# Transpositions behind two norms split between the next chunks, token halves at the norms and at the end, and alternating PSUM banks in a delta-rule and state-space block

## The chip, the core and the metric

The kernel runs on one core of a Trainium2 chip. The core has five engines with a queue of instructions each: TensorE (PE in the trace, its weight loads PEld), VectorE (DVE), ScalarE (ACT), GpSimd (POOL) and SyncE (SP, which here only issues transfers). They meet at semaphores. TensorE reads the on-chip memory SBUF and writes the accumulator memory PSUM; VectorE and ScalarE read both. The metric is the device time of one execution in microseconds; lower is better.

## The reference

One sequence of 256 tokens of width 2048 goes through two layers, in float32. The first is modulated by a conditioning vector: a gated delta-rule mixer (16 query/key heads, 32 value heads), a layer norm, a gated feed-forward block (FFN), a layer norm. The second is a hybrid: an RMS norm, eight projections, a short convolution branch and a state-space branch (s5), their mix, an output projection, the residual, and a last RMS norm.

```python
mod = (cond @ mod_w[i] + mod_b[i])[:, None, :]
sh1, sc1, ga1, sh2, sc2, ga2 = jnp.split(mod, 6, axis=-1)
h = x * (1 + sc1) + sh1
y = gated_deltanet(h, ...)                  # ends with o @ gdn_w_out
x = layer_norm(ALPHA_DN * x + (1 + ga1) * y, ln_g[i, 0], ln_b[i, 0])
h = x * (1 + sc2) + sh2
y = swiglu(h, ffn_w_gu[i], ffn_w_down[i])
x = layer_norm(ALPHA_DN * x + (1 + ga2) * y, ln_g[i, 1], ln_b[i, 1])
...
h = rmsnorm(x, norm_g)
proj = jnp.einsum('bld,dn->bln', h, w_in)
v, bg, cg, za, u, zb, ga, gb = jnp.split(proj, SPLITS, axis=-1)
...
m = jax.nn.sigmoid(ga) * ya + jax.nn.sigmoid(gb) * yb
x = x + jnp.einsum('bld,de->ble', m, w_o)
return rmsnorm(x, final_g)
```

## The kernel before, in words

Every product is made to float32 accuracy from three products of shorter numbers: a weight and an activation are each split into a high part (`wh`, `hh`) and a low part (`wl`, `hl`), and high x high, high x low and low x high are summed in PSUM. Weights stream through four buffers in **chunks** of 2 x 128 rows by 512 columns. SyncE loads a chunk into `wr`, ScalarE copies its high part (`high`, L1582; in the delta loop `gh`, L1391), VectorE subtracts for its low part (`low`, L2059; in the delta loop GpSimd does it, L595), and TensorE multiplies. A chunk that gives tokens on partitions (`tchunk`) takes 12 matmuls of 512 columns, six for each half of 128 tokens; one that gives channels on partitions (`chunk`) takes 24 of 256 columns. The semaphores s_hc, s_lc and s_ck count high parts, low parts and used chunks. `stream` on ScalarE and VectorE runs three chunks ahead and has events hung between the chunks.

PSUM is four tensors of 1024 columns, two banks each: pg0, pg1, pd0, pd1.

**Delta loop.** The projections of head block g (8 blocks, 24 chunks each: q and k, then v, then z) run beside the delta rule of block g-1. Before each of most chunks TensorE takes one step of the delta rule, which waits for VectorE and ScalarE. q and k gather in pg0, v in pg1, z in pg0 again (in block 0 z goes to pd1). ScalarE copies z out at the turn to the next block (`z_out`, L1439), and the next block's first chunk waits for it, since it writes pg0 as well. VectorE and ScalarE run six of these blocks in a hardware loop, TensorE's are written out. VectorE also forms columns of the modulation from tiles of `mod_w` (L1818, L1820), which GpSimd's queue loads between its low parts.

**Output projection and first norm.** The 40 chunks of `w_out` (numbers 0 to 39, `CK_FF` = 40) fill four blocks of 512 output columns; the last is chunks 24 to 39 in pg1. Small work is hung between them: at chunk 38 TensorE transposes 16 tiles (`bbar`), which ScalarE copies (`prep3`). After chunk 39 TensorE spreads the modulation ga2 over the partitions (`row_of`, L1146), while VectorE scales the last block by ga1, adds the residual, takes the statistics and the mean and variance (`scaled`, `stats`, `mean_var`). ScalarE makes the inverse deviation from a logarithm and an exponential (`inv_std`), VectorE normalizes four blocks of 512 columns (L2256), TensorE transposes each (`flip`, 8 tiles a block, 32 in all, into pd0 and pd1 by turns), ScalarE scales and shifts them on the way out of PSUM (`lift`, L1662), and VectorE splits them into high and low (`split_up`, L2114 and L2115). Then the FFN's first chunk starts.

**Second norm.** The FFN's last down-projection ends in four blocks (`down_last`), each scaled, added and measured. Before each, VectorE makes two low parts, chunks of the hybrid's projection among them. Then follow inverse deviation, scale and shift in tokens (L2309, L2311), ScalarE's squares for the RMS norm (L1683), the second normalization (L2318), `flip`, `lift` and `split_up` as before. The hybrid's first 32 chunks (u and zb) are a hardware loop of two passes on TensorE and ScalarE; ScalarE counts up the loop's start semaphores after the last `lift`.

**End.** `w_o` is 32 chunks into pd0 and pd1 by turns. After the last chunk VectorE adds the last 512 columns of both token halves (L2437), ScalarE squares (L1763), VectorE sums (L2440), ScalarE takes the root, VectorE multiplies four parts of 1024 columns (L2445) and SyncE stores each.

What sets the order around the change is the order in which the code stands on each engine, and the semaphores; there is no planner.

## Time and profile before

| what | value |
|---|---|
| median of 3 runs | 2849.15 us (2848.85 to 2851.08) |
| the profiled execution | 2848.96 us, its span 2847.0 us |
| mean granted clock of TensorE | 0.986 of full speed |
| TensorE busy | 2720.7 us, 96% of the span |
| VectorE, ScalarE, GpSimd busy | 1949.3, 1208.2, 812.5 us |
| read from HBM | 548.19 MB, 193 GB/s over the span |

The span runs from the first to the last instruction of the traced execution. Busy times of the engines overlap. Where TensorE idles, the trace names the instruction that it waited for. A wait for several semaphores is put down to the one that came last.

### The profile page before, as it was taken

How to read it: one execution, taken by the hardware profiler on the slowest of the kernel's cores; microseconds unless marked ns; L12 is line 12 of the kernel's file. 1: busy time of each engine (PE TensorE's matmuls, PEld its weight loads, DVE VectorE, ACT ScalarE, POOL GpSimd, SP SyncE). 2: the span in 40 equal slices, each digit the busy share in tenths (PEclk: the TensorE clock that was granted, in tenths of full speed). 3: DMA queues.
4: the chain of work that ended last, by engine and by line, in shares of the span. 5: the costliest groups of instructions: out<-in, count | busy, mean ns of one | idle time of the engine just before them, and what ended most of it. 6: DMA issues, size and time to landing. Idle time of an engine off the chain costs nothing.

```text
span 2847.0 us, 51314 instructions
## 1 busy us (share of the span) xinstructions
PE 2720.7 (96%) x20214; PEld 2404.2 (84%) x20214; DVE 1949.3 (68%) x2285; ACT 1208.2 (42%) x1521; POOL 812.5 (29%) x554
## 2 busy tenths in 40 slices
PE   6999999999997999999999999969999999999998
PEld 4788988898895777888888888769899999999996
DVE  1377877787778677666666666676999898555554
ACT  2255455545544444333333333344333334433343
POOL 1066666666667510000000000001555552000000
PEclk8999999999999999999999999989999999999999
DMA  9866666676665666666665555535554555555554
GB/s 364 311 195 214 223 216 200 205 247 199 200 223 169 212 184 207 187 191 189 188 188 187 189 189 186 167 115 169 156 171 148 157 169 172 179 185 183 184 201 147
DMA packets 283920, 552.72 MB, mean 194 GB/s; under 512 B 16817, under 2 KB 54258, under 8 KB 282610
## 3 DMA queue, kind: packets, MB, share of 16 engines
q1 hardware_dynamic: 263632, 474.02, 52.7%
q0 software_dynamic: 19408, 76.06, 7.2%
q8 instruction: 130, 2.13, 0.3%
q10 hardware_dynamic: 722, 0.28, 0.0%
q14 instruction: 28, 0.23, 0.0%
HBM read 548.19 MB, written 2.10 MB: 193 GB/s over the span
## 4 chain that ended last, share of the span: by engine, by line
PE 79%; DVE 11%; ACT 4%; issue 2%; DMA 2%; POOL 1%; DVEq 0%; SPq 0%; ACTq 0%; POOLq 0%; PEld 0%
PE pg L1130 20%; PE pg L1117 14%; PE pg L821 13%; PE pd L1130 11%; PE pd L1117 7%; PE pg L812 4%; DVE wl L2059 2%; PE pd L736 2%; DMA arena<-in_mod_w 1%; DVE arena L2340 1%; PE pd L985 1%; DVE arena L2342 1%; PE pd L1003 1%; DVE arena L2335 1%; PE pg L842 1%
## 5 line engine op out<-in xcount | busy, mean ns | idle before, releaser
L2059 DVE TENSOR_TENSOR wl<-wr,wh 128x1024 fp32r<-128x1024 f32 x616 | 773.0, 1264 | 515.7 <-ACT wh L1582 512.5
L1582 ACT ACTIVATE wh<-wr 128x1024 fp32r<-128x1024 f32 x616 | 652.6, 1060 | 1004.8 <-PE pg L1117 344.6
L595 POOL TENSOR_TENSOR wl<-wr,wh 128x1024 fp32r<-128x1024 f32 x195 | 479.8, 2462 | 394.3 <-ACT wh L1391 394.1
L1117 PE MATMUL pg<-hh,wh 128*128 128x256 f32 x1536 | 438.4, 285 | 3.9 <-ACT arena L1700 2.5
L1117 PE MATMUL pg<-hl,wh 128*128 128x256 f32 x1536 | 434.6, 283 | 0.0
L1117 PE MATMUL pg<-hh,wl 128*128 128x256 f32 x1536 | 434.3, 283 | 0.0
L1391 ACT ACTIVATE wh<-wr 128x1024 fp32r<-128x1024 f32 x216 | 227.7, 1057 | 349.3 <-PE pg L821 219.9
L821 PE MATMUL pg<-hh,wh 128*128 128x256 f32 x1024 | 301.2, 294 | 14.8 <-ACT arena L1439 12.0
L1117 PEld LDWEIGHTS pg<-hh,wh 128*128 128x128 f32 x1536 | 294.4, 192 | 16.6 <-issue 13.6
L1820 DVE SCALAR_TENSOR_TENSOR arena<-arena,condt 128x512 f32<-128x512 f32 x240 | 282.4, 1177 | 32.4 <-DMA arena<-in_mod_w 26.9
L1117 PEld LDWEIGHTS pg<-hl,wh 128*128 128x128 f32 x1536 | 294.5, 192 | 0.0
L1117 PEld LDWEIGHTS pg<-hh,wl 128*128 128x128 f32 x1536 | 294.4, 192 | 0.0
L821 PE MATMUL pg<-hl,wh 128*128 128x256 f32 x1024 | 290.1, 283 | 0.0
L821 PE MATMUL pg<-hh,wl 128*128 128x256 f32 x1024 | 290.1, 283 | 0.0
L1130 PE MATMUL pg<-wh,hh 128*128 128x512 f32 x704 | 276.8, 393 | 0.0
L1130 PE MATMUL pg<-wl,hh 128*128 128x512 f32 x704 | 276.1, 392 | 0.0
L1130 PE MATMUL pg<-wh,hl 128*128 128x512 f32 x704 | 275.3, 391 | 0.0
L725 POOL COPY arena<-arena 128x256 f32 x8 | 6.4, 798 | 875.5 <-ACT arena L1700 875.5
L821 PEld LDWEIGHTS pg<-hh,wh 128*128 128x128 f32 x1024 | 196.5, 192 | 33.1 <-ACT arena L1439 14.6
L821 PEld LDWEIGHTS pg<-hl,wh 128*128 128x128 f32 x1024 | 196.8, 192 | 0.2 <-issue 0.2
L821 PEld LDWEIGHTS pg<-hh,wl 128*128 128x128 f32 x1024 | 196.6, 192 | 0.0
L1130 PEld LDWEIGHTS pg<-wh,hl 128*128 128x128 f32 x704 | 132.3, 188 | 29.4
(392 smaller groups left out, 5323.6 us busy)
## 6 DMA issues: line engine op xcount, KB each, us to landing
wr<-in_w_in SPq DMA_DIRECT2D x224, 512.0 KB, 3.9
wr<-in_ffn_w_gu SPq DMA_DIRECT2D x176, 512.0 KB, 4.4
wr<-in_gdn_w_in SPq DMA_DIRECT2D x128, 512.0 KB, 4.3
arena<-in_mod_w POOLq DMA_DIRECT2D x64, 1024.0 KB, 7.7
wr<-in_ffn_w_down SPq DMA_DIRECT2D x88, 512.0 KB, 3.6
arena<-in_mod_w SPq DMA_DIRECT2D x32, 1024.0 KB, 12.2
wr<-in_gdn_w_in SPq DMA_DIRECT2D x128, 256.0 KB, 2.9
wr<-in_gdn_w_out SPq DMA_DIRECT2D x56, 512.0 KB, 4.6
```

What stands on the lines that cost most here:

```text
L595: nc.gpsimd.tensor_tensor(wl[c % RING][:], wraw[c % 4], wh[c % RING][:].bitcast(F32), ALU.subtract)\
L736: return nc.tensor.transpose(dst, src, ident[0:n, 0:n])
L812: m = nc.tensor.matmul(halves(bank)[:, t, :], h_s[x][:, 2 * kp + k, t * P:(t + 1) * P], w[c % RING][:, k, :], skip_group_check=True, start ...
L821: m = nc.tensor.matmul(bank[:, n * T:(n + 1) * T], w[c % RING][:, k, n * P:(n + 1) * P], h_s[x][:, 2 * kp + k, :], skip_group_check=True, ...
L842: m = nc.tensor.matmul(halves(pg[g])[:, h, :], o_s[x][:, 2 * kp + k, h * P:(h + 1) * P], w[c % RING][:, k, :], skip_group_check=True, star ...
L985: m = nc.tensor.matmul(block(pd[par], *crossed(s, b, n)), lTb[r, n, r], Tc[r, n, :], start=True, stop=True)
L1117: m = nc.tensor.matmul(bank[:, n * T:(n + 1) * T], w[s][:, k, n * P:(n + 1) * P], act[x][:, k0 + k, :], skip_group_check=True, start=(firs ...
L1130: m = nc.tensor.matmul(halves(bank)[:, h, :], act[x][:, k0 + k, h * P:(h + 1) * P], w[s][:, k, :], skip_group_check=True, start=(first and ...
L1391: a(wh[c % RING][:], wraw[c % 4], ACT.Copy).then_inc(s_hi, 1)
L1582: a(wh[c % 4][:], wraw[c % 4], ACT.Copy).then_inc(s_hc, 1)
L1820: m = stt(out=dst, in0=mw[t % 2][:, k, :], scalar=condt[:, kk:kk + 1], in1=dst, op0=ALU.mult, op1=ALU.add)
L2059: v.tensor_tensor(wl[c % 4][:], wraw[c % 4], wh[c % 4][:].bitcast(F32), ALU.subtract).then_inc(s_lc, 1)
```

## The change

**Banks by turns in the delta loop.** `group_bank` gives the three groups of block g the banks 0, 1, 0 for odd g and 1, 0, 1 for even g from 2 on; block 0 is as before. A block's first chunk then waits for the convolution of the block before, and only its ninth for the z copy. ScalarE's and VectorE's hardware loops hold two blocks a pass.

**Token halves at the first norm.** The last four chunks of `w_out` are run for token half 0 first, all four, then for half 1. VectorE adds, measures and normalizes half 0 beside the second halves. ga2's rows move to chunk 30.

**Pieces at both norms.** The transposed blocks are cut into five pieces (0 and 1 are halves of block 0). TensorE transposes pieces 0 to 2 ahead of the first chunk of the next projection, piece 3 behind the first chunk and piece 4 behind the second. Low and high parts of the next chunks move in between. The hybrid's first loop is written out on TensorE and ScalarE, and the start semaphores are counted up ahead of the lifts.

**Token halves at the end.** The last four chunks of `w_o` run half 0 first; half 0 is squared, scaled and stored in part beside the second halves; the last store is 512 columns wide.

```diff
+LAST_OUT = 36
+OUT_PARTS = ((0, 0, 1024), (0, 1024, 2048), (1, 0, 1024), (1, 1024, 1536), (1, 1536, 2048))
+PIECES = ((0, 0, 2), (0, 2, 4), (1, 0, 4), (2, 0, 4), (3, 0, 4))
+def pieces_for(t):
+    return t + 1 if t < 2 else t // 2 + 2
+def first_bank(g):
+    return 0 if g == 0 else (g + 1) % 2
+        def group_bank(g, grp):
+            return pg[(first_bank(g) + grp) % 2]
...
@@ TensorE, gchunk @@
-                if c == 0 and not first_g:
+                if c == 0 and g == 1:
+                    pe.wait_ge(s_zo, 1)
+                    pe.wait_ge(s_cd, 1)
+                elif c == 0 and not first_g:
+                    pe.wait_ge(s_cd, g * 2)
+                if c == 8 and g == 1:
+                    pe.wait_ge(s_cd, 2)
+                elif c == 8 and not first_g:
                     pe.wait_ge(s_zo, g)
-                    pe.wait_ge(s_cd, g * 2 - 1)
-                if c == 8 and not first_g:
-                    pe.wait_ge(s_cd, g * 2)
...
@@ TensorE, the chunks of w_out @@
-                tchunk(0, 0, t, pg[g % 2], o_s, 2 * k, g >= 2 and k == 0, last)
+                if t < LAST_OUT:
+                    tchunk(0, 0, t, pg[g % 2], o_s, 2 * k, g >= 2 and k == 0, last)
+                elif t == LAST_OUT:
+                    for n in range(LAST_OUT, CK_FF):
+                        pe.wait_ge(s_lc, n + 5)
+                        m = half_chunk(n, 0, pg[1], o_s, 2 * out_chunk(n)[1], False, n == CK_FF - 1)
+                    m.then_inc(s_oh0, 1)
+                if t >= LAST_OUT:
+                    half_chunk(t, 1, pg[1], o_s, 2 * k, False, last).then_inc(s_ck, 1)
...
+                if t == 30:
+                    pe.wait_ge(s_ap, 4)
+                    pe.wait_ge(s_ev, 3)
+                    row_of(pg[0], 5 * KD)
+                    row_of(pd[1], 5 * KD + 8).then_inc(s_pp, 1)
...
-            flip(0, res)
+            flip(0, res, (0, 1, 2))
...
+            def first_need(n, src, t):
+                if t in (1, 2):
+                    flip(n, src, (t + 2,))
+                pe.wait_ge(s_hn, 5 * n + pieces_for(t))
...
-            flip(1, xs)
-            with pe.Fori(0, 2) as j:
+            flip(1, xs, (0, 1, 2))
+            for j in range(2):
                 for i in range(2):
                     pe.wait_ge(s_uz, j * 2 + (i + 1))
-                    group(j, 16, CK_HYB + 8 * i, pg[i], h_s, 8, lambda t: pe.wait_ge(s_hn, 5 + t // 2))
+                    group(j, 16, CK_HYB + 8 * i, pg[i], h_s, 8,
+                          (lambda t: first_need(1, xs, t)) if j == 0 and i == 0 else None)
...
@@ ScalarE @@
-            with act.Fori(0, NIT - 2) as j:
-                beside(j)
-                turn(j)
+            with act.Fori(0, (NIT - 2) // 2) as i:
+                for odd in range(2):
+                    beside(i * 2 + odd, odd)
+                    turn(i * 2 + odd, odd)
...
             def prep3():
-                act.wait_ge(s_pp, 5)
+                inv_std(1, 0, 1)
+                act.wait_ge(s_pp, 6)
...
-                for c in range(4):
-                    act.wait_ge(s_tr, 4 * n + c + 1)
+                for i, (c, first, end) in enumerate(PIECES):
+                    act.wait_ge(s_tr, 5 * n + i + 1)
...
+                    if i in (2, 3):
+                        high(0, 0, c0 + i - 2 + AHEAD)
...
+            for sem in (s_uz, s_uz, s_za, s_gb):
+                act.sem_inc(sem, 1)
-            inv_std(2)
+            inv_std(3, 0, TT)
...
-            with act.Fori(0, 2) as j:
-                stream(j, 16, CK_HYB, 16, {7: lambda: out_u(j), 15: lambda: out_zb(j)})
+            for j in range(2):
+                stream(j, 16, CK_HYB, 16, {7: lambda: out_u(j), 15: lambda: out_zb(j)}, 0 if j else 2)
...
@@ VectorE, first norm @@
+            def last_half(t):
+                bank, row, part = halves(pg[1])[:, t, :], ga1_row[:, 1536:D], res[:, t, 1536:D]
+                link(v.tensor_tensor(bank, bank, row, ALU.mult))
+                m = stt(out=part, in0=part, scalar=ALPHA, in1=bank, op0=ALU.mult, op1=ALU.add)
...
+                link(v.bn_stats(bst[:, t, 3, :], part))
+                mean_var(t, t + 1)
...
+            dve.wait_ge(s_oh0, 1)
+            last_half(0)
+            low(0, 0, CK_FF)
             dve.wait_ge(s_rs, 1)
             for c in range(4):
-                for t in range(TT):
...
+                normed(0, 512 * c, 512 * (c + 1))
+            low(0, 0, CK_FF + 1)
+            used(0, 0, CK_FF - 1)
+            last_half(1)
+            dve.wait_ge(s_rs, 2)
+            for c, first, end in PIECES:
+                normed(1, 512 * c + P * first, 512 * c + P * end).then_inc(s_xn, 1)
+            low(0, 0, CK_FF + 2)
+            split_up(0, (sg, hgt), CK_FF)
...
@@ VectorE, second norm @@
-            stream(0, 0, CK_FD, 8, {1 + 2 * n: (lambda n=n: down_last(n)) for n in range(4)})
+            stream(0, 0, CK_FD, 6, {1 + 2 * n: (lambda n=n: down_last(n)) for n in range(3)})
+            down_last(3)
...
+            low(0, 0, CK_HYB + 1)
             dve.wait_ge(s_x2, 4)
...
+            low(0, 0, CK_HYB + 2)
+            split_up(1, htmp, CK_HYB)
...
@@ the end: TensorE, ScalarE, VectorE @@
+            for c in range(CK_END - 4, CK_END):
+                pe.wait_ge(s_lc, c + 5)
+                m = half_chunk(c, 0, pd[1], m_s, 2 * (c - CK_O - 24), False, c == CK_END - 1)
+            m.then_inc(s_oh0, 1)
+            for c in range(CK_END - 4, CK_END):
+                half_chunk(c, 1, pd[1], m_s, 2 * (c - CK_O - 24), False, c == CK_END - 1).then_inc(s_ck, 1)
...
+            for t in range(TT):
+                squares_o(3, t, t + 1)
+                act.sem_inc(s_sq, 1)
+                act.wait_ge(s_mv, 4 + t)
+                link(a(rs[:, t:t + 1], mv[:, t, 0:1], ACT.Ln, scale=1.0 / D, bias=cst[:, 0:1]))
+                a(rs[:, t:t + 1], rs[:, t:t + 1], ACT.Exp, scale=-0.5).then_inc(s_rs, 1)
...
+            dve.wait_ge(s_oh0, 2)
+            add_half(0)
+            mean_square(0)
             dve.wait_ge(s_be, 16)
...
+            final(0)
+            used(0, 0, CK_END - 1)
+            add_half(1)
+            final(1)
+            mean_square(1)
+            for i in range(2, len(OUT_PARTS)):
+                final(i)
```

TensorE at the turn from block 2 to block 3: `pg0<-wh,hh` and `pg0<-hh,wh` name the bank written and the two operands. Before, the last rows of block 2 and the first of block 3:

```order
L812 MATMUL pg0<-wh2_59,hh_53 128x512
L812 MATMUL pg0<-wl2_63,hh_53 128x512
L812 MATMUL pg0<-wh2_59,hl_54 128x512
L821 MATMUL pg0<-hh_53,wh0_57 128x256
L821 MATMUL pg0<-hl_54,wh0_57 128x256
```

and after:

```order
L833 MATMUL pg1<-wh2_59,hh_53 128x512
L833 MATMUL pg1<-wl2_63,hh_53 128x512
L833 MATMUL pg1<-wh2_59,hl_54 128x512
L842 MATMUL pg0<-hh_53,wh0_57 128x256
L842 MATMUL pg0<-hl_54,wh0_57 128x256
```

No instruction moved; z, which the last rows of the block form, now lies in the bank that the next block's first rows leave alone.

VectorE at the first norm, from the last low part before the statistics to the first split. `wl<-wr,wh` is a low part, the rows `128x512 x8` are the normalization, `hh` and `hl` the split. Before:

```order
L2059 TENSOR_TENSOR wl_63<-wr,wh_59 128x1024
L2101 TENSOR_TENSOR pg<-pg,arena 128x1024
L2246 SCALAR_TENSOR_TENSOR arena<-arena,pg 128x2x512
L2105 BN_STATS arena<-arena 128x6 x2
L2109 BN_AGGR arena<-arena 128x2 x2
L2256 TENSOR_SCALAR arena<-arena 128x512 x8
L2114 CAST hh<-arena 128x1024
```

and after, from the statistics of half 0 on:

```order
L2321 BN_STATS arena<-arena 128x6
L2166 BN_AGGR arena<-arena 128x2
L2116 TENSOR_TENSOR wl_61<-wr,wh_57 128x1024
L2327 TENSOR_SCALAR arena<-arena 128x512 x4
L2116 TENSOR_TENSOR wl_62<-wr,wh_58 128x1024
L2314 TENSOR_TENSOR pg<-pg,arena 128x512
L2315 SCALAR_TENSOR_TENSOR arena<-arena,pg 128x512
L2321 BN_STATS arena<-arena 128x6
L2166 BN_AGGR arena<-arena 128x2
L2327 TENSOR_SCALAR arena<-arena 128x256 x2
L2327 TENSOR_SCALAR arena<-arena 128x512 x3
L2116 TENSOR_TENSOR wl_63<-wr,wh_59 128x1024
```

The same arithmetic stands twice at half the width, with the low parts of three chunks between its steps.

VectorE ahead of the second norm, the last two blocks of the down projection: `pd<-pd,arena` scales a block. Before:

```order
L2101 TENSOR_TENSOR pd<-pd,arena 128x1024
L2287 TENSOR_TENSOR arena<-arena,pd 128x2x512
L2105 BN_STATS arena<-arena 128x6 x2
L2059 TENSOR_TENSOR wl_62<-wr,wh_58 128x1024
L2059 TENSOR_TENSOR wl_63<-wr,wh_59 128x1024
L2101 TENSOR_TENSOR pd<-pd,arena 128x1024
L2287 TENSOR_TENSOR arena<-arena,pd 128x2x512
```

and after:

```order
L2158 TENSOR_TENSOR pd<-pd,arena 128x1024
L2372 TENSOR_TENSOR arena<-arena,pd 128x2x512
L2162 BN_STATS arena<-arena 128x6 x2
L2158 TENSOR_TENSOR pd<-pd,arena 128x1024
L2372 TENSOR_TENSOR arena<-arena,pd 128x2x512
L2162 BN_STATS arena<-arena 128x6 x2
L2166 BN_AGGR arena<-arena 128x2 x2
```

The two low parts between the blocks are gone from here; one stands behind the four pairs that scale and shift in tokens, the other behind the second normalization.

## Rows read from the trace of the kernel before

**Rows 1.** The page: span, section 1, and a line of section 5 (columns: busy us, mean ns).
```profile
span 2847.0 us, 51314 instructions
...
PE 2720.7 (96%) x20214; PEld 2404.2 (84%) x20214; DVE 1949.3 (68%) x2285; ACT 1208.2 (42%) x1521; POOL 812.5 (29%) x554
...
L1582 ACT ACTIVATE wh<-wr 128x1024 fp32r<-128x1024 f32 x616 | 652.6, 1060 | 1004.8 <-PE pg L1117 344.6
```

**Rows 2.** Waits of TensorE over the span: us in total, times, longest.
```profile
PE pg L821 <- ACT arena L1439: 12.0, 6, 2.0
...
PE pg L1117 <- ACT arena L1700: 2.5, 1, 2.5
```

**Rows 3.** Timelines of TensorE and VectorE at turns: start us, us, instruction, [idle before].
```profile
266.32 0.39 PE L821 MATMUL pg<-hh,wh 128*128 128x256 f32 x1 [2.01 <-ACT arena L1439]
...
269.29 1.88 PE L916 MATMUL pd<-arena,ones 128*128 128x512 f32 x4
...
378.17 0.49 DVE L1818 TENSOR_SCALAR arena<-arena,condt 128x512 f32<-128x512 f32 x1 [0.31 <-DMA arena<-in_mod_w]
...
400.60 1.95 DVE L1820 SCALAR_TENSOR_TENSOR arena<-arena,condt 128x512 f32<-128x512 f32 x2 [1.16 <-DMA arena<-in_mod_w]
```

**Rows 4.** TensorE's longest wait in the last delta block, 859 to 965.
```profile
PE pd L934 <- DVE arena L1933: 6.7, 1, 6.7
```

**Rows 5.** Timelines at the first norm: TensorE, VectorE, ScalarE.
```profile
1100.68 1.95 PE L1146 MATMUL pg<-ident,modt 128*128 128x128 f32 x16
1102.46 1.95 PE L1146 MATMUL pd<-ident,modt 128*128 128x128 f32 x16
...
1114.14 1.06 PE L736 MATMUL pd<-ident,arena 128*128 128x128 f32 x8 [0.76 <-ACT arena L1662]
1114.96 0.48 PE L1130 MATMUL pg<-wh,hh 128*128 128x512 f32 x1
...
1104.64 1.42 DVE L2105 BATCH_NORM_STATS2 arena<-arena 128x6 f32<-128x512 f32 x2
...
1107.17 3.74 DVE L2256 TENSOR_SCALAR arena<-arena 128x512 f32<-128x512 f32 x8 [0.69 <-ACT arena L1648]
...
1106.60 0.30 ACT L1647 ACTIVATE arena<-arena,cst 128x2 f32<-128x2 f32 x1 [0.21 <-DVE arena L2109]
...
1110.23 3.76 ACT L1662 ACTIVATE arena<-pd,arena 128x256 f32<-128x256 f32 x8 [3.10 <-PE pd L736]
```

**Rows 6.** Timelines at the second norm: VectorE, then TensorE.
```profile
1857.81 2.36 DVE L2059 TENSOR_TENSOR wl<-wr,wh 128x1024 fp32r<-128x1024 f32 x2
1860.09 1.23 DVE L2101 TENSOR_TENSOR pd<-pd,arena 128x1024 f32<-128x1024 f32 x1
...
1877.20 3.26 DVE L2318 TENSOR_SCALAR arena<-arena 128x512 f32<-128x512 f32 x8 [1.91 <-ACT arena L1687]
1881.74 0.69 DVE L2114 CAST hh<-arena 128x1024 fp32r<-128x1024 f32 x1 [1.28 <-ACT arena L1660]
...
1878.13 5.27 PE L736 MATMUL pd<-ident,arena 128*128 128x128 f32 x24 [20.30 <-DVE arena L2318]
...
1885.90 0.38 PE L1117 MATMUL pg<-hh,wh 128*128 128x256 f32 x1 [1.27 <-ACTq L1692]
```

**Rows 7.** A stretch of 1 us: each engine's busy us (instructions), then PEclk, DMA share, GB/s.
```profile
1882.00:1883.00 1.00, 1.00 (x6) 1.00 (x7) 0.97 (x2) 1.00 (x4) 0.00 (x0) 0.57 0.00 0
```

**Rows 8.** ScalarE's table load ahead of the second Silu of the hybrid block.
```profile
1977.89 1.28 ACT L1700 ACT_TABLE_LOAD   x1 [1.83 <-PE pg L1117]
```

**Rows 9.** The end: chain of waits, VectorE's timeline, and the DMA issues.
```profile
2814.93 20.19 PE pd L1130 x88
...
2837.21 0.73 ACT arena L1763 x2
...
2838.77 4.87 DVE L2445 SCALAR_TENSOR_TENSOR arena<-arena,xT 128x1024 f32<-128x1024 f32 x4 [0.60 <-ACT arena L1770]
...
out<-arena SPq DMA_DIRECT2D x4, 512.0 KB, 2.8
```

More of the change, by code:

```diff
@@ L573, in _ @@
                 loads(0, 0, CK_O + 8 * g, w_o, 512 * g, 8)
-            for i in range(2 * TT):
+            for i, (t, first, end) in enumerate(OUT_PARTS):
                 sp.wait_ge(s_fin, i + 1)
-                t, half = i // 2, slice((i % 2) * 1024, (i % 2 + 1) * 1024)
-                sp.dma_start(out[0, t * P:(t + 1) * P, half], res[:, t, half]).then_inc(s_out, 16)
-            sp.wait_ge(s_out, 32 * TT)
+                sp.dma_start(out[0, t * P:(t + 1) * P, first:end], res[:, t, first:end]).then_inc(s_out, 16)
+            sp.wait_ge(s_out, 16 * len(OUT_PARTS))
         @block.gpsimd
@@ L804, in gchunk @@
                 pe.wait_ge(s_low, g * NCH + (c + 5))
-                bank, first, last = pg[grp % 2], kp == 0, kp == 7
-                if first_g and grp == 2:
-                    bank = pd[1]
+                bank, first, last = pd[1] if first_g and grp == 2 else group_bank(g, grp), kp == 0, kp == 7
                 if grp == 2:
@@ L1198, in _, with flip @@
                     m.then_inc(s_pp, 1)
-            def flip(n, src):
-                for c in range(4):
-                    pe.wait_ge(s_xn, 4 * n + c + 1)
+            def flip(n, src, pieces):
+                for i in pieces:
+                    c, first, end = PIECES[i]
+                    pe.wait_ge(s_xn, 5 * n + i + 1)
                     if c == 1 and n == 0:
@@ L1206, in flip @@
                     if c >= 2:
-                        pe.wait_ge(s_hx, 4 * n + c - 1)
-                    for k in range(4):
+                        pe.wait_ge(s_hx, 5 * n + c)
+                    for k in range(first, end):
                         for h in range(TT):
@@ L1569, in beside, with turn @@
                     pass
-            def turn(j, more=None):
-                z_out(j + 1)
+            def turn(j, odd, more=None):
+                z_out(j + 1, group_bank(1 + odd, 2))
                 if more:
@@ L1582, in high, with stream @@
                 a(wh[c % 4][:], wraw[c % 4], ACT.Copy).then_inc(s_hc, 1)
-            def stream(j, per, c, n, events={}):
-                for t in range(n):
+            def stream(j, per, c, n, events={}, start=0):
+                for t in range(start, n):
                     if not (isinstance(j, int) and c + t + AHEAD >= CK_END):
@@ L1914, in _ @@
             squares(0)
-            for _ in conv(0, 1):
+            for _ in conv(0, 1, group_bank(0, 1)):
                 pass
@@ L2105, in stats, with mean_var @@
                     link(v.bn_stats(bst[:, t, g, :], res[:, t, 512 * g:512 * (g + 1)]))
-            def mean_var():
-                for t in range(TT):
+            def mean_var(first=0, end=TT):
+                for t in range(first, end):
                     m = v.bn_aggr(mv[:, t, :], bst[:, t].rearrange("p a b -> p (a b)"))
```

195 lines of the change are left out of this document (100 added, 95 removed).

## The prediction, made before the changed kernel had run

> **What bounds the kernel now.** I read the share table first: TensorE is busy for 96% of a span of 2847.0 us [rows 1]. So an edit pays only where TensorE stands still, or behind its last matmul. The table of waits names these places. The reader should see in it one line that counts six equal waits, 12.0 us together, of a projection matmul for ScalarE's copy of a PSUM bank at L1439, and one of 2.5 us for the Silu at L1700 [rows 2]. The timelines give the rest: both norms, where TensorE waits for a chain over VectorE and ScalarE, and the end. I took each in turn and followed the chain instruction by instruction. "Chunk" is one k-pair of a weight block.
>
> **Turns of the delta loop: 12.0 us.** At a turn, ScalarE copies the z block out of pg0, and the next projection, which writes pg0 too, starts at 266.32 after 2.01 us of idle behind that copy [rows 3]. After the change the next block writes the other bank, which the convolution left long before; the copy is asked for only eight chunks later. A chunk lasts 269.29 - 266.32 = 2.97 us [rows 3], so the copy has over 20 us. In six turns (into blocks 2 to 7) the wait goes; the turns into block 1 and into the output projection keep theirs, as the latter starts on pg0, which holds z. Sum: 6 x 2.0 = 12.0 us.
> What is late next? TensorE now comes 2.0 us earlier to VectorE's results, but the first mod_w tile is issued behind GpSimd's low part of chunk 2, which hangs on ScalarE's z copy and its next weight copy, neither of which moves. VectorE already waited 0.31 us for that tile at 378.17 and will wait 2.3 [rows 3]. So for some 20 us VectorE runs with up to 2 us less of a lead. At 400.60 it waits 1.16 us for a tile whose issue hangs on TensorE's chunks [rows 3]: there the whole schedule is 2 us earlier and the lead is back. I count no loss. The bounds are 0 and 12 us given back. Loop bodies on ScalarE and VectorE are twice as long with half the passes; I take that at nothing, covered by the same eight chunks on ScalarE.
>
> **First norm: 1.2 us, less the clock.** Before: the last chunk ends at 1100.68, where the ga2 rows begin, and the first FFN matmul is at 1114.96 [rows 5], so 14.3 us. The rows (16 matmuls, until 1104.4) and all 32 transpositions lie within it. After, with T0 the end of the four first halves:
> - The second halves take 24 x 0.229 = 5.5 us (88 matmuls in 20.19 us, [rows 9]) and 16 transpositions of bbar 1.9 us between them: T1 = T0 + 7.4.
> - VectorE on half 0: multiply and add at 512 columns are half of 1.23 [rows 6], statistics 0.71, aggregate 0.2: T0 + 2.3. ScalarE takes inv_std only behind the weight copy of chunk 41, which waits for chunk 37's second half: 2.75 + 1.06 [rows 1] and two small ops of 0.3 and 0.2 [rows 5], T0 + 4.4. Then four normalizations of 0.47 [rows 5] and a low part of 1.2 [rows 6]: T0 + 7.6. That is just behind T1, so half 0 costs no more than 0.2 us.
> - Half 1: 2.3 + 0.6, five pieces in 1.9, the low part of chunk 42 1.2 (it stands ahead of the split), the split of the first piece, half of 0.69 + 1.23 [rows 6], 1.0. Transposition and ScalarE's lift of that piece (two of eight that take 3.76, [rows 5]) end before. FFN starts at T1 + 0.2 + 7.0, some 7.3.
> - Exposed besides: the ga2 rows, moved to chunk 30, 3.7 us, which VectorE had hidden; and two groups of eight transpositions behind FFN chunks 0 and 1, 1.07 each at full clock [rows 5], 2.1 together. They wait for nothing: their pieces were normalized before, and the pd bank they use was lifted.
> 7.3 + 3.7 + 2.1 = 13.1 against 14.3. Bounds: -1.5 (a loss) and +2 us.
>
> **Second norm: 3.0 us, less the clock.** Before, two low parts start at 1857.81 and hold VectorE 2.36 us, so the last down block is scaled at 1860.09, though TensorE was done at 1857.8 [rows 6]. After, they stand behind the second normalization's arithmetic and behind the pieces: the whole chain comes 2.2 us earlier. The first moved one fills the 1.9 us in which VectorE waits for ScalarE [rows 6]; the second, 1.2 us, delays the split: pieces start at 1875.0 instead of 1877.20, take 3.5, low part 1.2, split of the half piece 1.0: 1880.9. The hybrid projection started at 1885.90, behind the lift of all four and ScalarE's semaphore increments, which have moved ahead of it [rows 6]. Gain 5.0, minus two groups of transpositions now between chunks, 2.0: 3.0. Bounds 0 and 4.
>
> **The clock at the norms: -2 us together.** Before the first matmul behind either norm TensorE has stood still for some time. The granted clock is then its lower level, 0.50 of full speed (1.2 GHz), and at the second norm it rises only during 1882-1883, of which it averages 0.57 [rows 7], after transpositions from 1878.13 on [rows 6]. So far the low clock touched only transpositions. Now fewer of them stand before the first chunk and idle time lies between, so part of a chunk may run at 1.2 GHz. A chunk at half speed costs 2.8 to 2.9 us more; I take 1.0 us at each norm, bounds 0 and 2.9.
> The Trainium skill ("TensorE: Matmul & The Clock Gate", What's actually happening) says that throttled is the default state and that activity releases it. The trace agrees: full clock returns only after TensorE has worked. By that rule the thinner row of transpositions releases it later; by the start of work alone it would be as before and the 2 us would stay.
>
> **Table load: 1.3 us.** The u/zb loop is written out twice on ScalarE, and in its order the second Silu has no table load. Before, the load at 1977.89 takes 1.28 us [rows 8], inside TensorE's wait of 2.5 us [rows 2]. Bounds 1.2 and 1.4.
> The skill's page "ScalarE: Activation LUTs" (What ACT_TABLE_LOAD costs) gives about 2.66 us, a drain included; by it the sum would be 1.4 us larger. The trace has the load end and the Silu begin at once, so I keep 1.3.
>
> **End: 3.6 us.** Before, the last matmul ends at 2814.93 + 20.19 = 2835.12, and the fourth final multiply at 2838.77 + 4.87 = 2843.64 [rows 9]: 8.5 us, then 3.4 to the span's end. After, token half 0 is squared, scaled and half stored during the last 5.5 us of matmuls. Behind the end: add 0.6; final(1), which stands ahead of the mean, 1.3; reduce 0.2 (ScalarE's squares, 0.73 [rows 9], end meanwhile); two small ops 0.5; multiplies 1.3 + 0.6 + 0.6, and 0.15 of hops: 5.25. The last store is 256 KB instead of 512, which landed in 2.8 [rows 9], and fewer queue before it: 3.1 instead of 3.4. Gain 3.3 + 0.3. Bounds 3.0 and 4.3.
>
> **Sum** against the profiled run's own 2848.96 us: 12.0 + 1.2 + 3.0 - 2.0 + 1.3 + 3.6 = 19.1, so 2829.9. The median of the shown runs, 2849.15, lies 0.2 above: 2830.
>
> **Rivals.**
> - *Slow chunks at both norms.* The clock stays at 1.2 GHz for the whole first chunk: 5.7 us instead of 2.0, 2834. For it: over 4 us of transpositions before the full clock at the second norm [rows 6, 7]. Against: 16 transpositions still stand ahead of the first chunk, and 24 were enough [rows 6].
> - *No clock loss,* and the first norm at its better bound: 2827.
> - *The turn's gain is eaten by VectorE.* The late mod_w tile pushes the chain until TensorE waits for it again, the place changed but not the time: 12 us back, 2842. For it: 0.31 us of wait there already. Against: not one TensorE wait on VectorE in those six blocks, and the idle 1.16 us at 400.60.
> - *Slower: the delta chain becomes TensorE's bound.* In the last block, where chunks are shorter, TensorE waits 6.7 us for one result of VectorE's [rows 4]. If the shifted VectorE brought that wait into each of six blocks, 6 x 6.7 = 40 us: 2870. It decides from (19.1 + 5.7) / 6 = 4.1 us of new waits per block on. Against: only 2 us are shifted.
>
> **Chances.** 0.2% is 5.7 us, about what a measurement of this kernel can tell from no change. Forecast 2830 with 0.65 (2828 to 2832), slow chunks 0.15, no clock loss 0.10, VectorE eats it 0.05 (still faster by 0.25%), slower 0.03, and 0.02 for that case with the norms giving nothing as well, within 0.2%. Faster 0.95, same 0.02, slower 0.03. Range 2825.5 to 2836.
>
> **What the changed profile would show.** Right: no TensorE wait on the z copy except into block 1 and the output projection, and each block 2.0 us shorter; eight transpositions after chunks 0 and 1 behind each norm; TensorE's wait at the second norm near 18 us, not 20.3 [rows 6], then short ones; one L1755 table load; the last final multiply 5.2 us behind the last matmul. A granted clock of 0.50 in the first chunk's stretch would set the norm terms lower. Wrong would be: new TensorE waits on VectorE's triangular steps after the turns, or VectorE's half 0 far behind T1, which would leave the first norm a loss.

## The result, and where the time went

| kernel | median | against the kernel before |
|---|---|---|
| before | 2849.28 us (20 runs) | |
| after | 2853.72 us (20 runs) | 1.0017, 95% interval 1.0011 to 1.0023 |

The change makes the kernel slower by 0.17%, at the edge of what can be told from nothing. 2830.0 had been forecast, 24 us below. One of the 20 runs of the kernel after took 4457.06 us at a mean granted clock of 0.556, and the ratio leaves it out. The profiled execution took 2852.55 us, its span is 3.6 us longer than before. First the page of the kernel after, to hold against [rows 1]: busy us, share, instructions.

```profile
span 2850.6 us, 51255 instructions
...
PE 2725.0 (96%) x20214; PEld 2408.0 (84%) x20214; DVE 1982.7 (70%) x2297; ACT 1203.9 (42%) x1522; POOL 807.1 (28%) x554
```

TensorE has the same instructions as before. VectorE has 12 more, because steps were cut into parts, and is busy 33 us longer. It got no more arithmetic to do, so the time must lie inside instructions that stand still. The waits of TensorE come next (us in total, times, longest), to hold against [rows 2, 4, 6].

```profile
PE pd L955 <- DVE arena L1989: 21.8, 7, 6.7
PE pd L755 <- DVE arena L2405: 17.9, 1, 17.9
PE pd L1321 <- DVE arena L2434: 13.0, 8, 1.9
...
PE pd L1006 <- DVE arena L2019: 1.6, 3, 0.5
PE pg L1138 <- ACT arena L1755: 1.1, 1, 1.1
```

The six waits on the z copy (12.0 us) are gone, as forecast. In their place the Gram products (L955) wait in each of six blocks, 2.3 to 2.6 us each, for VectorE's scaling of q and k (L1989). The seventh wait of that row is the 6.7 us of [rows 4].

Following one instruction after another at the same point of the program in both traces gives a ledger. The lag is how much later the kernel after is there.

| point of the program | lag, us | step |
|---|---|---|
| z copy into block 1 | 0.0 | |
| first chunk of the output projection | +10.3 | turns +10.3 |
| its chunk 29 | +8.9 | the lower clock lasts longer in before, -1.4 |
| its last chunk | +12.5 | ga2 rows +3.5 |
| first Silu of the FFN | +9.4 | first norm -3.1 |
| last down-projection chunk | +10.5 | longer low clock in after, +1.1 |
| end of the first 32 hybrid chunks | +7.1 | second norm -3.4 |
| behind the second Silu | +5.7 | table load -1.4 |
| last matmul | +7.1 | state loop +1.4 |
| last final multiply | +3.8 | end -3.3 |
| end of the span | +3.6 | end -0.2 |

Only the first step is far from its forecast, by 22 us. It shows in one instruction: the first of the three copies (of 8, 8 and 16 numbers a partition) with which VectorE fetches the convolution's taps for the next block (`taps`; L1844 before, L1900 after). These are the rows of that line in both kernels (min/median/max ns, first and last start).

```profile
L1844 DVE COPY arena<-vc x8: 173/1376/1519, 16.4 to 767.9; 128x8 f32 x6, 128x8 f32<-128x8 f32 x2
```

```profile
L1900 DVE COPY arena<-vc x8: 171/5982/6096, 16.4 to 774.8; 128x8 f32 x6, 128x8 f32<-128x8 f32 x2
```

The copy needs 0.17 us, took 1.4 before and takes 6.0 now. The timelines at the turn into block 3 tell why. Before (start us, us; VectorE, then GpSimd):

```profile
372.60 1.37 DVE L1844 COPY arena<-vc 128x8 f32 x1 [0.18 <-DVE arena L1927]
...
371.51 2.42 POOL L595 TENSOR_TENSOR wl<-wr,wh 128x1024 fp32r<-128x1024 f32 x1
374.92 3.12 POOL L595 TENSOR_TENSOR wl<-wr,wh 128x1024 fp32r<-128x1024 f32 x1 [1.00 <-ACT wh L1391]
```

After (VectorE, GpSimd, TensorE):

```profile
372.37 5.98 DVE L1900 COPY arena<-vc 128x8 f32 x1 [0.18 <-DVE arena L1983]
378.95 1.23 DVE L1989 TENSOR_TENSOR arena<-arena 128x1024 f32<-128x1024 f32 x1
...
372.03 1.54 POOL L608 DMA_DIRECT2D arena<-in_mod_w  x2
373.59 4.72 POOL L614 TENSOR_TENSOR wl<-wr,wh 128x1024 fp32r<-128x1024 f32 x2
...
380.24 2.72 PE L955 MATMUL pd<-arena 128*128 128x128 f32 x16 [2.58 <-DVE arena L1989]
```

Before, the copy ended at 373.97, when GpSimd's low part ended (373.93) and GpSimd then had to wait 1.00 us for ScalarE's next high part. After, it ended at 378.35, when the second of two low parts ended (378.31). At this turn TensorE's chunks are at the same time in both traces, within 0.25 us. Relative to them the z copy is 2.0 us later, since TensorE no longer waits for it. GpSimd's chain hangs on the z copy, so these low parts start 2.1 us later; the next high part hangs on TensorE and starts 0.2 us earlier. So the idle microsecond between two low parts, through which the copy had slipped, is closed. The same shift also lets the copy begin ahead of the row of low parts, during the issue of the two loads, instead of beside a low part; no run here separates the two. The q/k scaling behind the copy comes 2.6 us later than TensorE now wants it.

The Trainium skill ("SBUF — State Buffer", Who interferes with whom) says that VectorE and GpSimd share one pair of ports and that whoever starts first holds it for the whole instruction; on VectorE's side this concerns copies in a mode that uses both ports, and steps with two operands from SBUF while GpSimd reads SBUF. The trace agrees on who is blocked. By that rule the copy would have been let through behind the first low part, at about 376.0; it stood until the second had ended. What held the copy from 372.37 to 373.57, beside the issue of two loads, no run here shows: in e4 below it took 0.45 us beside the same issue.

The wait also has a price in the clock. The granted clock fell to 0.50 for about 3 us around the Gram products in three of the six blocks (from 279.0, 381.4 and 582.8 on), where the kernel before stays at 1.00; here is one stretch of 1 us from the kernel after (busy us of PE, PEld, DVE, ACT, POOL, then the clock, DMA share, GB/s).

```profile
382.00:383.00 1.00, 1.00 (x7) 1.00 (x7) 0.96 (x3) 0.72 (x1) 0.00 (x0) 0.50 0.92 335
```

The 16 matmuls at 380.24 take 2.72 us where the same 16 took 1.95 before. These three blocks fall back by 2.0 to 2.2 us each, the other three by 1.1 to 1.4.

The last delta block has the same picture, before and after alike. Here VectorE's scaling of q and k itself is in the queue behind GpSimd (VectorE, GpSimd's last of four subtractions in a row from 879.72 on, TensorE):

```profile
879.35 10.76 DVE L1989 TENSOR_TENSOR arena<-arena 128x1024 f32<-128x1024 f32 x1 [4.97 <-ACT arena L1518]
...
886.69 2.33 POOL L614 TENSOR_TENSOR wl<-wr,wh 128x1024 fp32r<-128x1024 f32 x1
...
890.16 1.23 PE L955 MATMUL pd<-arena 128*128 128x128 f32 x4 [6.72 <-DVE arena L1989]
```

A step of 1.2 us took 10.8. VectorE is not always held for the whole row, though. Further on in the same block of the kernel before, the masking pair gets in between two of GpSimd's subtractions that stand back to back:

```profile
885.60 4.22 DVE L1953 TENSOR_TENSOR arena<-arena,m1t 64x512 f32<-64x512 f32 x2
...
886.40 2.87 POOL L595 TENSOR_TENSOR wl<-wr,wh 128x1024 fp32r<-128x1024 f32 x1
889.23 2.86 POOL L648 TENSOR_TENSOR ol<-arena,oh 128x1024 fp32r<-128x1024 f32 x1
```

The pair ends at 889.82, half a microsecond behind the end of the first of them, and the second takes 2.86 us instead of 2.4. The six copies and the scaling in the kernel after all began while GpSimd was issuing loads, this pair beside a subtraction; but in e3 the last block's scaling began beside one too and stood for 9.07 us, through three more. What decides between the two cases is open.

The 10.8 us step is behind the 6.7 us row which the prediction quoted [rows 4], without asking how long the instruction waited for had taken.

### The profile page after: what moved, and what is told of

Same layout as the page of the kernel before. It is cut to its first block, busy times and chain, and to the rows that moved or that the text cites. A ratio compares the mean times of both kernels' runs of the same rounds, so it can differ in the third digit from the quotient of the medians.

```text
span 2850.6 us, 51255 instructions
## 1 busy us (share of the span) xinstructions
PE 2725.0 (96%) x20214; PEld 2408.0 (84%) x20214; DVE 1982.7 (70%) x2297; ACT 1203.9 (42%) x1522; POOL 807.1 (28%) x554
## 4 chain that ended last, share of the span: by engine, by line
PE 79%; DVE 13%; DMA 2%; issue 2%; ACT 1%; POOL 1%; DVEq 0%; SPq 0%; ACTq 0%; POOLq 0%; PEld 0%
PE pg L1149 20%; PE pg L1138 14%; PE pd L1149 12%; PE pg L842 10%; PE pd L1138 7%; PE pg L833 5%; DVE wl L2116 2%; DMA arena<-in_mod_w 2%; PE pd L755 2%; DVE arena L1900 1%; DVE arena L1876 1%; DVE arena L2428 1%; PE pd L1006 1%; DVE arena L2430 1%; PE pd L1024 1%
## 5 line engine op out<-in xcount | busy, mean ns | idle before, releaser
L1149 PEld LDWEIGHTS pg<-wh,hh 128*128 128x128 f32 x704 | 132.6, 188 | 31.4 <-DVE hl L2172 2.1
```

What stands on the lines that cost most here:

```text
L1149: m = nc.tensor.matmul(halves(bank)[:, h, :], act[x][:, k0 + k, h * P:(h + 1) * P], w[s][:, k, :], skip_group_check=True, start=(first and ...
```

## The experiments

### e1 and e2: the two halves of the change apart

e1 is the kernel before with `group_bank`, its waits and the doubled loops. e2 is the kernel after with this undone:

```diff
 def first_bank(g):
-    return 0 if g == 0 else (g + 1) % 2
+    return 0
...
-                elif c == 0 and not first_g:
-                    pe.wait_ge(s_cd, g * 2)
+                if c == 0 and not first_g:
+                    pe.wait_ge(s_zo, g)
+                    pe.wait_ge(s_cd, g * 2 - 1)
...
```

> The kernel before with only the turn part of the change: banks alternate from block to block, with the waits and the doubled loops that go with it; norms, table load and end as before. Theory 'blocked copy': in the changed kernel each of six blocks loses 3.6 us (a wait of 2.6 us for VectorE's q/k scaling, 0.3 and 0.6 us behind it) against 2.0 us gained at the z copy, so about +10 us here: 2859.5 (2858 to 2861), with VectorE's first tap copy of a block at 6.0 us instead of 1.4. By my prediction's own sum this kernel would be at 2837. If the loss came from the norm parts instead, it would be at 2837 as well.

> The changed kernel with the banks fixed as before and the projection's waits on z and on the convolution as before; the doubled loop bodies stay. From the two traces the other parts should be worth: first norm -0.2, second norm with the last down block -3.1, table load 0 net, end -3.5, together -6.8: 2842.5 (2841.5 to 2844). Six tap copies at 1.4 us again, six waits of 2.0 us on the z copy back. If doubled loop bodies cost something, it is slower than that by their price (my prediction took it at nothing).

Measured: e1 2859.81 us, ratio 1.0039 (1.0025 to 1.0052); e2 2842.45 us, ratio 0.9973 (0.9964 to 0.9983). Both within 0.4 us of what was expected. In e1 the row of the tap copy reads as in the kernel after:

```profile
L1855 DVE COPY arena<-vc x8: 173/5992/6129, 16.5 to 774.8; 128x8 f32 x6, 128x8 f32<-128x8 f32 x2
```

So the banks cost 10.4 us by themselves, the rest of the change is worth 7.0, and the doubled loop bodies, which e2 kept, cost nothing: in its trace the six blocks are within 0.1 us of the kernel before.

### e3: the copies moved away

```diff
+            link(taps(1))
...
-                if mods:
-                    done(taps(it + 1))
-                else:
-                    dve.sem_inc(s_v, 1)
+                dve.sem_inc(s_v, 1)
...
                 for h in range(VH):
                     m = stt(out=rhs1[:, h, :], ...)
                 done(m)
+                if more:
+                    link(taps(it + 2))
```

> The changed kernel with the three tap copies of a block moved on VectorE from the block's start to behind the rhs1 step of the block before, where VectorE is idle for 6.9 us. Theory 'the copy itself is slow' (its dynamic address, not what runs beside it): the whole turn gain is back, 2832. Theory 'blocked by GpSimd': the q/k scaling, which reads two SBUF operands, takes the copy's place, starts while GpSimd issues the two mod_w loads and stands still until the two low parts behind them end, so the block's wait shrinks only from 2.6 to about 1.9 us: 2850 (2847 to 2852), with a q/k scaling of over 6 us in the trace. Theory 'late mod_w tile': 2853, no change.

Measured: 2847.33 us, ratio 0.9992 (0.9983 to 1.0001), at the lower end of the second theory's range. The next block's rows show it (VectorE, GpSimd): the scaling of q and k now stands where the copy stood.

```profile
470.15 6.97 DVE L1987 TENSOR_TENSOR arena<-arena 128x1024 f32<-128x1024 f32 x1 [0.24 <-ACT arena L1518]
...
471.30 4.73 POOL L614 TENSOR_TENSOR wl<-wr,wh 128x1024 fp32r<-128x1024 f32 x2
```

It ends 1.1 us behind GpSimd's row, about its own length of 1.2. The copy itself is not slow: the step that takes its place ahead of that row of low parts is held as well. The waits at L955 fell from 21.8 to 15.8 us, of which the last block gave 1.7, and in the six blocks the clock fell once instead of three times.

### e4 and e5: GpSimd leaves a gap, VectorE untouched

```diff
                 for t in range(2):
                     mod_load(it * 8 + 32, t)
+                if not o_low:
+                    pool.wait_ge(s_v, it * len(VO) + VO["qkn"])
```

GpSimd's low parts behind the two loads wait for VectorE's scaling of q and k.

e5 has the wait without the `if`, so in the last block too.

> The changed kernel with one wait more, on GpSimd: in the seven loop blocks it starts the low part behind the two mod_w loads only when VectorE's q/k scaling of that block is done. VectorE's program is untouched. Theory 'blocked by GpSimd': the tap copy takes under 1.5 us, the q/k scaling 1.2, the new wait of the gram products is gone and all 3.6 us a block come back, 2832 (2831 to 2836). Theory 'the copy itself is slow': it still takes 6.0 us and the low parts now come behind it, 2854 or more. Theory 'late mod_w tile': 2853, since no load moves.

Measured: 2837.63 us, ratio 0.9963 (0.9949 to 0.9977). One wait added, on an engine that TensorE hardly waits for, wins 16 us against the kernel after. VectorE's copy and scaling (first two rows), and GpSimd behind them:

```profile
468.17 0.45 DVE L1902 COPY arena<-vc 128x8 f32 x1 [0.16 <-DVE arena L1985]
...
469.21 1.23 DVE L1991 TENSOR_TENSOR arena<-arena 128x1024 f32<-128x1024 f32 x1
...
481.19 4.60 DVE L2011 TENSOR_TENSOR arena<-arena,m1t 64x512 f32<-64x512 f32 x2
```

```profile
470.63 7.08 POOL L614 TENSOR_TENSOR wl<-wr,wh 128x1024 fp32r<-128x1024 f32 x3 [1.24 <-ACT wh L1445]
479.97 2.40 POOL L614 TENSOR_TENSOR wl<-wr,wh 128x1024 fp32r<-128x1024 f32 x1 [2.26 <-ACT wh L1445]
```

The copy takes 0.45 us, the scaling 1.23, and the wait at the Gram products is gone. It came out 5.6 us above the 2832 expected and outside the range. The trace names a wait that fits: the masking pair (L2011) falls beside a low part and takes 4.60 us, where the same pair took 1.63 in the kernel before and 4.34 in the kernel after. Here TensorE waits for it:

```profile
PE pd L989 <- DVE arena L2011: 9.1, 7, 1.3
```

In this trace the clock does not fall in the six blocks, and each is 0.9 us shorter than before: 5.4 us are won of the 12.0 forecast.

> The kernel with the one wait on GpSimd (low parts behind the two mod_w loads wait for VectorE's q/k scaling), now in the last delta block as well. In that block the q/k scaling took 10.8 us instead of 1.2 beside a row of GpSimd's subtractions without a gap, and TensorE waited 6.7 us for it, before and after the change alike. Theory 'blocked by GpSimd': it takes under 1.5 us there too, the 6.7 us wait goes and nothing takes its place: 6 to 7 us below the run with the gap in the loop blocks alone, 2831 (2828 to 2834). Theory 'that wait has another cause' (ScalarE's exponents, chunks of the output projection): no difference, 2837.6.

Measured: 2835.68 us, ratio 0.9953 (0.9939 to 0.9966). In the last block the scaling takes 1.23 us at 865.51 and its wait is gone. But 2835.68 is outside the expected range, and the intervals of e4 and e5 overlap, so no gain of e5 over e4 is shown. GpSimd is late with the low parts now (2.4 us in e4, 5.3 here):

```profile
PE pg L864 <- POOL wl L614: 5.3, 3, 2.5
```

TensorE's waits in the last block are 2.8 us shorter than in e4, yet the block is 1.1 us longer in the trace; more of its matmuls run at the lower clock.

### e6: a second gap, and e7: TensorE kept busy at the first norm

e6 has the gap of e5, the copies of e3, and ahead of the low part of chunk 6:

```diff
+                    if t == 4:
+                        pool.wait_ge(s_v, it * len(VO) + VO["lm"])
                     low(it + 1, t + 2)
```

> The gap in all blocks, the tap copies moved into VectorE's idle 6.9 us of the block before, and a second wait on GpSimd: the low part of chunk 6 waits for VectorE's masking of the Gram blocks (the pair of 64x512 multiplies), which in the run with one gap took 4.6 us for two beside GpSimd and which TensorE then waited for 1.3 us in each of six blocks. Theory 'blocked by GpSimd': these waits go (8 us) with the 6.7 of the last block: 2823 (2820 to 2827), the masking pair at 1.7 us. Rival 'GpSimd becomes late': held back 2.8 us longer, it is late with the low part of chunk 6 and TensorE waits for that instead: 2831.

Measured: 2841.99 us, ratio 0.9978 (0.9969 to 0.9987), worse than with one gap. The masking pair takes 1.39 us, as meant. But three low parts then run in a row, 7.99 us, and TensorE waits longer on the levels of the triangular inverse behind it, which nobody had expected:

```profile
PE pd L1027 <- DVE arena L2028: 15.0, 8, 2.3
```

e7 is e6 with these transpositions of no use:

```diff
+            pe.wait_ge(s_ev, 4)
+            fill(16)
             flip(0, res, (0, 1, 2))
+            fill(14)
```

> The kernel with both gaps and the moved tap copies, plus 30 transpositions of no use on TensorE in its idle time at the first norm (16 ahead of the row of 16 useful ones, 14 behind it), into a bank that is free. Nothing they write is read. In the changed kernel the granted clock fell to 0.50 at 1122 us and stayed there until 1125.3, so the first FFN chunk lasted 4.3 us instead of 2.7. If the clock follows TensorE's idle time ahead of it, the chunk is at full speed and 1.5 us are won against the kernel without them; in the time that is 0.05%, below what the comparison can tell, so the trace decides: mean granted clock of the first chunk 1.00 against 0.6 or so. If the clock fell for something else, the chunk stays at 4.3 us and the time is up to 0.3 us longer.

Measured: 2842.58 us, ratio 0.9977 (0.9967 to 0.9986), no difference in the time, as expected. What is left are the rows of TensorE and the granted clock. After (TensorE; then stretches of 1 us with busy us of PE, PEld, DVE, ACT, POOL, the clock, DMA share, GB/s):

```profile
1117.14 1.94 PE L755 MATMUL pd<-ident,arena 128*128 128x128 f32 x16 [3.73 <-DVE arena L2327]
1120.94 0.50 PE L1149 MATMUL pg<-wh,hh 128*128 128x512 f32 x1 [1.86 <-DVE hl L2172]
...
1122.00:1123.00 1.00, 1.00 (x4) 0.81 (x3) 0.96 (x2) 0.51 (x1) 0.00 (x0) 0.56 1.01 426
1123.00:1124.00 1.00, 1.00 (x4) 0.72 (x3) 1.00 (x2) 0.00 (x0) 0.00 (x0) 0.50 1.00 420
```

With the fillers:

```profile
1112.75 1.69 PE L758 MATMUL pg<-ident 128*128 128x128 f32 x14
1114.84 0.50 PE L1152 MATMUL pg<-wh,hh 128*128 128x512 f32 x1 [0.39 <-DVE hl L2182]
...
1115.00:1116.00 1.00, 1.00 (x5) 0.82 (x6) 0.97 (x3) 1.00 (x2) 0.00 (x0) 1.00 0.97 410
1116.00:1117.00 1.00, 1.00 (x6) 0.82 (x5) 0.96 (x2) 0.36 (x1) 0.00 (x0) 1.00 1.03 434
```

From the first FFN chunk's start to that of the second group of transpositions behind it took 8.1 us after, 7.4 in e6 and 6.5 in e7. The lower level cost 1.6 us in the kernel after. In e7 no stretch between 1104 and 1122 is below 1.00, which fits a clock that follows TensorE's idle time. But it is one trace of each kernel, and the low stretch moves by itself: in e6, the nearest kernel without the fillers, it lies at 1106 to 1112.8, over the transpositions and the start of the chunk. So the cause is not shown.

### e8: the table load alone

The u/zb loop written out twice in the kernel before (`for j in range(2)` on TensorE and ScalarE), in one execution.

> The kernel before with one edit: the two passes over u and zb written out twice on TensorE and on ScalarE. One look, for the trace. My prediction: the table load of 1.3 us inside TensorE's wait of 2.5 us goes and 1.3 us are won to the end. Theory from the two traces: the Silu's wait shrinks to 1.1, but the first state products wait for VectorE, which does not come earlier, so the 1.4 us are back by the first quarter of the state loop: waits on VectorE's L2346 of 13.0 to 13.5 us instead of 11.8, and a span of 2847 instead of 2845.6.

Measured: 2845.91 us, span 2844.0. The Silu's wait is 1.1 us, but my theory fell: the waits on L2346 stayed at 11.9 us,

```profile
PE pd L1277 <- DVE arena L2346: 11.9, 8, 2.0
PE pd L1117 <- ACT arena L1742: 1.7, 1, 1.7
PE pg L1117 <- ACT arena L1700: 1.1, 1, 1.1
```

and the 1.4 us gained at the Silu were still there at the end of the state loop. Most of the other 1.7 us of the span arose at 1006 to 1009, where the kernel before still ran at a clock of 0.50 and e8 at 1.00; the 1.5 us less of waiting in the one row of [rows 4] (5.2 us here) were lost again to the clock within the same block. So in this one trace the prediction's term holds. What took 1.4 us back in the kernel after is something else: TensorE waits 1.75 us for VectorE at 2093.89, where it had waited 0.24. (A fall of the granted clock at 2013 to 2016 costs 1.5 us, but the kernel before has one like it at 2060 to 2063.) e2 has the same wait of 1.75 us, at 2190.21. Why it came, no run here shows.

### e9 to e12: the order on VectorE, the gap without the change, the gap again

e9 is e5 with VectorE's half sums of the mod_w tiles one step later in each loop block (`if t: mods(j * 8 + 32, t - 1)`); e10 has e3's copies as well; e11 is the kernel before with e5's gap; e12 is e5 once more.

> The changed kernel with GpSimd's gap in all blocks and one edit on VectorE: in the loop blocks each half sum of a mod_w tile comes one step later. In the run with the gap alone VectorE stood 3.7 us ahead of its decay-and-mask multiply for the block's first mod_w tile, so the masking pair of 64x512 fell beside a low part, took 4.6 us instead of 1.6, and TensorE waited 1.3 us in each of six blocks (7.8). Theory: with the tile behind that pair the pair runs before GpSimd's next low part and the 7.8 us are won: 2828 (2825 to 2831) against the gap kernel beside it. Rival: the sums, one step later, are late for the loads they release, or the two-operand steps collide with another low part: TensorE waits elsewhere on VectorE or on a tile and the time stays at 2835 or above.

Measured: 2905.13 us, ratio 1.0191 (1.0178 to 1.0205), the rival's case and 70 us above its bound:

```profile
PE pd L756 <- DVE arena L2033: 38.5, 20, 3.4
...
PE pd L1065 <- DVE arena L2041: 10.8, 7, 2.4
PE pd L1037 <- DVE arena L2033: 10.2, 7, 1.6
```

TensorE waits on nearly every level of the inverse. The sums are the same instructions as in e5; a step later they stand ahead of those that TensorE waits for.

> The same with the tap copies moved into VectorE's idle time of the block before. The q/k scaling comes 1 us earlier, so GpSimd is held for less; TensorE waits for neither after the gap, so the theory expects no more than 1 us: 2827.5 (2825 to 2831). If the copies still hurt where they stand, it is 2 us or more ahead of the kernel without this edit.

Measured: 2900.69 us, ratio 1.0183 (1.0170 to 1.0196). With e9's order the base is lost, so it tells little of the copies.

> The kernel before with GpSimd's gap in all blocks and nothing of the change. TensorE did not wait for VectorE in its loop blocks, and the 2.0 us on the z copy stay, so nothing is to be won there; in the last block the 6.7 us wait goes and 2.9 us of waiting for the low parts come, as in the changed kernel. Theory: 2849.4 - 3.8 = 2845.6 (2843 to 2848), so the gap is worth about 4 us here against 18 beside the alternating banks. Rival: the gap is an improvement by itself, of the same size without the change: 2832. A gap that pushes the low parts onto VectorE's masking pair here too would cost up to 8 us back: 2849 or more.

Measured: 2856.34 us, ratio 1.0023 (1.0014 to 1.0032). The gap makes the kernel before slower and the kernel after faster: with the z wait in place TensorE does not wait for VectorE in the six blocks, and holding GpSimd for 3.3 us pushes its low parts onto the masking pair. All six z copy waits stay (12.0 us), and four new ones come:

```profile
PE pg L822 <- ACT arena L1440: 12.0, 6, 2.0
...
PE pd L967 <- DVE arena L1954: 5.1, 4, 1.3
```

In the trace the six blocks lose 9.6 us, 5.1 of them in these waits and most of the rest in three falls of the granted clock to 0.50; the last block wins 6.5.

> The kernel with the gap in all blocks once more, on the chip of the three others, so that they can be compared with it: 2835.7 as before (2833 to 2838).

Measured: 2835.69 us, ratio 0.9947 (0.9934 to 0.9960), the same as e5. This is the version that beats both kernels, by 14 us over before. Against e2, which leaves the banks out, it is 6.8 us faster, so the banks pay only together with the gap.

## Why the prediction was wrong

**Turns: forecast -12.0, measured +10.3.** The wait on the z copy went as forecast, 2.0 us in six blocks. The step that failed is "What is late next?", which asked it only of the mod_w tile and ended in "I count no loss". It followed VectorE's semaphores and left out that VectorE and GpSimd hinder each other without any. Moving TensorE 2 us earlier while GpSimd's chain stayed closed the idle microsecond between two low parts. Against the 12.0 us gained stand 22.3 us lost in the six blocks: 15.1 of waiting at the Gram products, 1.6 in three waits at a step behind them (L1006), and 5.6 in which TensorE ran slower, most of it at the granted clock of 0.50. That GpSimd would meet VectorE there could have been read before: 1.37 us for a copy of 8 numbers, ending where the low part ended, and 10.8 us for a step of 1.2. e1 shows the size, e3 that it isn't the copy, e4 that it is GpSimd's row. As to the mod_w tile, in the kernel after VectorE has no idle time ahead of its first mod_w step of these blocks. In e4 it waits 2.7 to 3.7 us for the tile and TensorE for nothing at the Gram products; whether that delay put the masking pair beside a low part, e9 was meant to show and could not.

**The rival that came nearest** is "Slower: the delta chain becomes TensorE's bound", which had 0.03. It named the kind of wait and the row, but had 6.7 us a block and 2870. By the prediction's own sum the gain is gone from 19.1 / 6 = 3.2 us a block on, and at 4.1 the kernel is slower by 0.2%; it was 3.7, a third more than the 2.8 of waits alone because of the clock, which this rival did not count. Its counter-argument, "only 2 us are shifted", failed because a shift of 2 us can change a duration by 4.6.

**First norm: forecast -1.2 and a clock loss of 1.0.** Measured are +3.5 for the ga2 rows (forecast 3.7) and -3.1 for the rest (forecast -4.9 + 1.0). The first FFN chunk starts 7.5 us behind the last chunk of the output projection, as worked out (7.3). The lower clock cost 1.6 us instead of 1.0 and is most of the difference: the norm part is 0.4 us of loss instead of 0.2 of gain.

**Second norm: forecast -3.0 and a clock loss of 1.0; measured -3.4.** TensorE's wait is 17.9 us ("near 18"), the hybrid starts 23.0 us behind the last down chunk instead of 28.1. The clock loss did not come:

```profile
1886.25 3.67 PE L755 MATMUL pd<-ident,arena 128*128 128x128 f32 x16 [17.89 <-DVE arena L2405]
1891.39 0.36 PE L1138 MATMUL pg<-hh,wh 128*128 128x256 f32 x1 [1.47 <-issue]
...
1889.00:1890.00 1.00, 0.93 (x5) 0.52 (x3) 1.00 (x2) 0.13 (x2) 0.00 (x0) 0.50 0.00 0
1890.00:1891.00 1.00, 0.00 (x0) 0.00 (x0) 0.97 (x3) 1.00 (x3) 0.00 (x0) 0.94 0.00 0
```

The 16 transpositions ran at 0.50, and the clock rose in the idle time ahead of the first chunk. The term of 2.0 us for both norms was right in sum (1.6) by luck, with one norm above its 1.0 us and one below.

**Table load: forecast -1.3, measured -1.4** at its place, and in the one execution of e8 it lasts.

**End: forecast -3.6, measured -3.5.** VectorE's rows and the stores, to hold against [rows 9]:

```profile
2842.26 0.69 DVE L2530 TENSOR_TENSOR arena<-arena,pd 128x512 f32<-128x512 f32 x1 [1.84 <-PE pd L1149]
...
2844.81 2.61 DVE L2539 SCALAR_TENSOR_TENSOR arena<-arena,xT 128x1024 f32<-128x1024 f32 x3 [0.60 <-ACT arena L1826]
...
out<-arena SPq DMA_DIRECT2D x3, 512.0 KB, 2.6
out<-arena SPq DMA_DIRECT2D x2, 256.0 KB, 2.7
```

The last multiply ends 5.20 us behind the last matmul (2842.22), where 5.25 had been worked out, and the span ends 3.2 us later (forecast 3.1).

The range of 2825.5 to 2836 was built from the bounds of the small terms. The largest term had bounds of 0 and 12 us given back and none for a loss, so it was the one that needed a row for its worst case.

## What to carry to other kernels

Before an engine's wait is taken away, look at how long the instructions of its partners last against the shortest of their kind, not only at who waits for whom: one that takes eight times its length and ends with another engine's instruction is a wait that no semaphore shows. Count also what a new wait does to the granted clock behind it. A shift of 2 us opens or closes such windows, in either direction, so a gain at one engine should be priced with the whole rows of VectorE and GpSimd laid side by side at their new times. A wait added to an engine with slack can be worth more than one removed from the bottleneck, but only beside the change that needs it.

## What the runs showed of the hardware that had not been expected

- A VectorE instruction blocked by GpSimd can stay blocked beyond the end of the GpSimd instruction: until two low parts had ended (6.0 us for a copy of 8 numbers that takes 0.17), or four (10.8 us for a step of 1.2). It need not: the masking pair at 885.60 in the kernel before got in between two subtractions in a row.
- GpSimd is hindered less the other way: a low part took 2.4 us alone and 2.9 to 3.1 where VectorE was at work first.
- Small steps suffer as much as large ones: the sum of four modulation columns (128x4) took 1.63 us at 362.87 in the kernel before, beside a low part, and 0.16 us at 477.37 in e9 without one.
- The granted clock fell to 0.50 inside running matmuls, 1.2 us after they had begun behind 1.9 us of idle time at the first norm, and around a wait of 2.6 us in three of six like blocks. It rose during idle time at the second norm.
- The same idle time of 2.0 us at each of six turns was followed by no fall of the clock in the kernel before, and by three in e11 (from 269, 570 and 771 on).
